# Scores of q and k from high and low parts: three fp32r matmuls in place of one fp32 matmul, twelve heads

## What is computed

```
qh = partial_rope(rms_norm(q.reshape(shp), q_norm_g), positions) * (HEAD_DIM ** -0.5)
kh = partial_rope(rms_norm(k.reshape(shp), k_norm_g), positions)
...
s = jnp.einsum('bnqrhe,bnkrhe->bnrhqk', qb, kn)
```

## Time and profile before

| | |
|---|---|
| time, median of 3 runs (lowest to highest) | 3410.15 us (3408.2 to 3416.05) |
| profiled execution, its own time | 3404.39 us |
| its span | 3403.1 us |
| busy: PE, DVE, ACT | 99%, 67%, 49% |
| heads' stretch of the trace | about 98 to 363 us |

### The profile page before, as it was taken

One profiled execution on the slowest core, in us unless ns is written; L12 is line 12 of the kernel. 1 busy time (PEld: TensorE's weight loads), 2 busy tenths in 40 slices (PEclk: granted clock), 3 DMA queues, 4 the chain that ended last, 5 costly groups with the idle time before them and its releaser, 6 DMA issues.

```text
span 3403.1 us, 66505 instructions
## 1 busy us (share of the span) xinstructions
PE 3372.4 (99%) x29362; PEld 3352.6 (99%) x29362; DVE 2284.4 (67%) x3021; ACT 1664.2 (49%) x1788; POOL 136.0 (4%) x132
## 2 busy tenths in 40 slices
PE   8999999999999999999999999999999999999999
PEld 8999999999999999999999999999999999999998
DVE  5777679986655555545555587778646778787456
ACT  5555434455544444343443454333445667777455
POOL 0000000144400000000000000000000000000000
PEclk9999999999999999999999999999999999999999
DMA  6435455566676666655566655555555545555543
GB/s 248 164 140 181 176 218 186 186 213 212 218 237 221 213 220 209 227 195 190 198 220 215 209 177 203 194 194 182 208 189 177 195 162 198 199 186 186 211 174 137
DMA packets 125328, 669.45 MB, mean 197 GB/s; under 512 B 11056, under 2 KB 44592, under 8 KB 47344
## 3 DMA queue, kind: packets, MB, share of 16 engines
q1 hardware_dynamic: 88224, 623.44, 52.2%
q10 hardware_dynamic: 36816, 41.75, 3.7%
HBM read 643.39 MB, written 20.97 MB: 195 GB/s over the span
## 4 chain that ended last, share of the span: by engine, by line
PE 94%; DVE 3%; ACT 1%; issue 1%; DMA 1%; ACTq 0%; SPq 0%; DVEq 0%
PE PS L553 30%; PE PS L554 30%; PE PS L555 30%; PE PS L848 2%; DVE WL L1538 1%; ACT WH L1039 1%; DMA RAW<-in_w_in 0%; DVE WX L1538 0%; DVE A L1562 0%; PE PS L743 0%; PE PS L728 0%; DVE OO L2081 0%; PE PS L568 0%; DVE XT L2087 0%; PE PS L830 0%
## 5 line engine op out<-in xcount | busy, mean ns | idle before, releaser
L1538 DVE TENSOR_TENSOR WL<-RAW,WH 128x2048 fp32r<-128x2048 f32 x579 | 1325.4, 2290 | 832.1 <-ACT WH L1039 829.9
L553 PE MATMUL PS<-A,WH 128*128 128x256 f32 x5536 | 1545.5, 279 | 18.2 <-DVE WL L1544 9.8
L554 PE MATMUL PS<-A,WH 128*128 128x256 f32 x5536 | 1532.1, 277 | 0.0
L555 PE MATMUL PS<-A,WL 128*128 128x256 f32 x5536 | 1531.9, 277 | 0.0
L1039 ACT ACTIVATE WH<-RAW 128x2048 fp32r<-128x2048 f32 x579 | 1107.6, 1914 | 846.4 <-PE PS L555 830.5
L553 PEld LDWEIGHTS PS<-A,WH 128*128 128x128 f32 x5536 | 1042.2, 188 | 23.0 <-DVE WL L1544 9.8
L554 PEld LDWEIGHTS PS<-A,WH 128*128 128x128 f32 x5536 | 1040.9, 188 | 0.6
L555 PEld LDWEIGHTS PS<-A,WL 128*128 128x128 f32 x5536 | 1040.4, 188 | 0.0
L553 PE MATMUL PS<-CO,WH 128*128 128x256 f32 x2048 | 565.2, 276 | 0.0
L554 PE MATMUL PS<-CO,WH 128*128 128x256 f32 x2048 | 565.2, 276 | 0.0
L555 PE MATMUL PS<-CO,WL 128*128 128x256 f32 x2048 | 565.2, 276 | 0.0
(11 more groups left out here) (294 smaller groups left out, 2903.9 us busy)
## 6 DMA issues: line engine op xcount, KB each, us to landing
RAW<-in_w_in SPq DMA_DIRECT2D x175, 1024.0 KB, 4.8
RAW<-in_peer_down SPq DMA_DIRECT2D x128, 1024.0 KB, 4.8
RAW<-in_peer_up SPq DMA_DIRECT2D x128, 1024.0 KB, 5.4
RAW<-in_w_out SPq DMA_DIRECT2D x80, 1024.0 KB, 4.7
RAW<-in_w_gate SPq DMA_DIRECT2D x32, 1024.0 KB, 4.8
RAW<-in_w_query SPq DMA_DIRECT2D x16, 1024.0 KB, 4.8
gates_away<-XT ACTq DMA_DIRECT2D x16, 1024.0 KB, 8.2
RAW<-in_pool_w SPq DMA_DIRECT2D x16, 1024.0 KB, 4.7
```

Source lines behind the costliest of these rows:

```text
L553: e.matmul(ps, wh, x[:, k, 0, :], start=first, stop=False, skip_group_check=True)
L554: e.matmul(ps, wh, x[:, k, 1, :], start=False, stop=False, skip_group_check=True)
L555: return e.matmul(ps, wl, x[:, k, 0, :], start=False, stop=last, skip_group_check=True)
L1538: e.tensor_tensor(W_LOW[c], RAW[:, c % NRAW, :], W_HIGH[c].bitcast(F32), ALU.subtract).then_inc(s_lo, 1)
```

## The change

The score step of each head no longer multiplies q and k as fp32. A new ACT step `qh` rounds the rotated q and k to fp32r in SQH; a new DVE step `ql` subtracts, which gives the low parts in SQL; `p2` then does three fp32r matmuls for each half of the queries, and waits for `ql` where it waited for `r3`. SQH and SQL are the buffers of the squares, so `sh` of the next head now waits for the scores of the head before. In `pe_out` the steps of head 11 and the split of chunk 3 move.

```diff
@@ att_pe
         if x == "p2":
-            e.wait_ge(AD[w].sem, AD[w].at(("r3", h)))
+            e.wait_ge(AD[w].sem, AD[w].at(("ql", h)))
             e.wait_ge(AA[w].sem, AA[w].at(("vn", h)))
             for qt in range(2):
-                ins = e.matmul(BANK[6][:, qt * T:qt * T + T], QKV[:, s, 0, qt * 128:qt * 128 + 128], QKV[:, s, 1, :],
-                               start=True, stop=True, skip_group_check=True)
+                for n, (q, k) in enumerate(((SQH, SQH), (SQH, SQL), (SQL, SQH))):
+                    ins = e.matmul(BANK[6][:, qt * T:qt * T + T], q[:, qt * 128:qt * 128 + 128], k[:, T:2 * T],
+                                   start=(n == 0), stop=(n == 2), skip_group_check=True)
@@ pe_out
-        parts = [(0, 0, 14), (1, 0, 14), (2, 0, 14), (3, 0, 6), (0, 14, 16), (1, 14, 16), (2, 14, 16), (3, 6, 16)]
+        parts = [(0, 0, 14), (1, 0, 14), (2, 0, 14), (3, 0, 9), (0, 14, 16), (1, 14, 16), (2, 14, 16), (3, 9, 16)]
...
-                if n == 28:
+                if n == 33:
                     att_pe(e, "p2", 11)
-                if n == 40:
+                if n == 44:
                     att_pe(e, "p3", 11)
-                if n == 44:
+                if n == 48:
                     att_pe(e, "p4", 11)
@@ att_act
             if h:
-                e.wait_ge(AP[1 - w].sem, AP[1 - w].at(("ss", h - 1)))
+                e.wait_ge(AP[1 - w].sem, AP[1 - w].at(("qk", h - 1)))
...
+        if x == "qh":
+            e.wait_ge(AD[w].sem, AD[w].at(("r3", h)))
+            e.activation(SQH[:, :].rearrange("p (a t) -> p a t", a=2), QKV[:, s, 0:2, :], ACT.Copy).then_inc(
+                AA[w].sem, AA[w].one(("qh", h)))
@@ act_first
                 if j == 0 and h >= 1:
                     att_act(e, "rt", h - 1)
+                if j == 1 and h >= 1:
+                    att_act(e, "qh", h - 1)
@@ att_dve
+        if x == "ql":
+            e.wait_ge(AA[w].sem, AA[w].at(("qh", h)))
+            e.tensor_tensor(SQL[:, :].rearrange("p (a t) -> p a t", a=2), qk,
+                            SQH[:, :].bitcast(F32).rearrange("p (a t) -> p a t", a=2), ALU.subtract).then_inc(
+                S.sem, S.one(("ql", h)))
@@ dve_first
                 if j == 0 and h >= 2:
                     att_dve(e, "rc", h - 2)
+                if j == 2 and h >= 1:
+                    att_dve(e, "ql", h - 1)
                 lo_to(e, c + 2)
```

More of the change, by code:

```diff
@@ L414, in build @@
     ap_n = two(("ss", "vt", "qk", "pt", "pv"))
-    aa_n = two(("sq", "sh", "ln", "rs", "vn", "e0", "e1", "pt"))
-    ad_n = two(("sl", "nq", "nk", "r1", "r2", "r3", "sm", "mx", "rc", "m0", "m1", "hi", "lo"))
+    aa_n = two(("sq", "sh", "ln", "rs", "vn", "qh", "e0", "e1", "pt"))
+    ad_n = two(("sl", "nq", "nk", "r1", "r2", "r3", "ql", "sm", "mx", "rc", "m0", "m1", "hi", "lo"))
     s_ones = sem("ones_rounded")
@@ L1199, in act_out @@
         hi_to(e, C_WO + 3)
+        att_act(e, "qh", 11)
         att_act(e, "ex", 11)
@@ L1780, in dve_out @@
         att_dve(e, "ro", 11)
+        att_dve(e, "ql", 11)
         att_dve(e, "sm", 11)
```

## The result

The changed kernel takes 3419.36 us in the median of 20 runs (3414.67 to 3426.43), the kernel before on the same chip 3413.55 (3406.49 to 3422.58, 20 runs). The ratio is 1.0020 with a 95% interval of 1.0013 to 1.0027: slower by 6.8 us (4.4 to 9.2). Measured a second time, in eight new runs, it was 3415.87 us, ratio 1.0026 (1.0015 to 1.0036), or 8.9 us (5.1 to 12.3). One of ten executions of the kernel before in that second session took 5200.5 us at a granted clock of 0.61 and is left out of every comparison.

What follows compares the result with a forecast made beforehand. PE, busy in 3372.4 of 3403.1 us, bounds the kernel. Waits less work 4.2, ring 2.0, carried lateness 1.9, weight loads 0.6 and tail 0.7 make +9.4 us: 3419.5 us from a median of 3410.15, range 3413 to 3426.

Steps and rivals of the forecast that it cites:

- The ring: Heads 9 to 11: ACT and DVE alternate in a 20.5 us loop, outside PE's 19.45 us period; +2.0 us.
- Waits at the scores: Heads 0 to 10: PE waits for q and k, ready later behind qh and ql; 6.5 us in sum.
- PE's work: Scores cost PE 0.69 us a head against 0.88, -2.3 us; weight loads not hidden at waits, +0.6 us.
- The tail: End of pe_out: the chunk after the first four has three blocks less cover and waits; +0.7 us.
- Carried lateness: Heads before the ring binds: lateness is carried on in part from head to head; +1.9 us.
- Waits alone: Rival: no ring binds, only score waits and small terms cost; +4.2 to +5.5 us, 3414 to 3416; chance 0.20.
- All hidden: Rival: q and k ready when PE needs them, only the 2.3 us work gain counts; 3407.9 us; chance 0.06.
- Ring and GLA: Rival: in heads 3 to 8 GLA's steps add a 1 us wait in each; +15 us, 3425; chance 0.10.
- The clock: Rival: short repeated idling drops PE to 1.2 GHz for one head, up to 19 us, 3439; chance 0.03.

Runs made afterwards that it cites:

- the run with the product alone: Kernel before with the scores made by six fp32r matmuls a head on the normalised input, no qh, ql or new wait; ratio 1.0004.
- the run with another bank: Changed kernel with PSUM banks of the output projection's first and fourth chunks swapped; 283.11 us from head 0's first q evacuation to the output projection's transposes, one execution.
- the one with the longer ring: Changed kernel with an unused ACT copy of 0.6 us behind the exponentials of each head; ratio 1.0023.
- the new steps alone: Changed kernel with qh and ql computed and waited for, but the scores again fp32 products of q and k; ratio 1.0029.

## Why the prediction was right, and where a step was off

The forecast was 3419.5 us, slower by 9.4; measured were 3419.36 us and ratios that make 6.8 and 8.9 us, and 8.84 and 9.03 in two pairs of traces. That the time itself is met to 0.2 us is luck: in the same 20 runs the kernel before took 3413.55 us, 3.4 more than the 3410.15 that the forecast started from, and the difference of the two medians is 5.8 us and not 9.4. The first ratio's interval ends at 9.2. The direction and the mechanism hold, and by the traces the sum does to 0.6 us. The terms hold less well than the sum.

- **The ring: right.** Forecast 20.5 us, measured 20.40, and the missing 0.1 is the start of the high part 0.54 us behind `qh` where 0.66 was taken. It binds from head 8 to 9 on, as forecast. Four runs stand behind it: the period ignores PE's work, grows with an ACT copy inside the ring, outlasts a later place of the scores, and vanishes when `qh` stands one place further back on ACT.
- **Waits at the scores: right in kind, high in size.** Heads 0 and 5 wait longest, as forecast, and seven steps wait where "some ten" were forecast; 6.9 us lies at the low end of 7 to 10. In terms of the sum, the idle time forecast was 6.5 + 2.0 + 1.9 + 0.7 = 11.1 us; PE's idle time grew by 8.04. Some 1.5 us of the difference is only where it is counted: the forecast goes by starts, the profile lets a wait begin when the last matmul's record ends, 0.28 us after its start, where without a wait the next one starts after 0.12. The other 1.6 us are waits that came out short, head 1's 0.1 for 0.4 and those of heads 9 and 10 among them. A slip of the sum goes the other way: the ring's term takes off a wait of 0.6 us for each of heads 9, 10 and 11, but at head 11 none had been counted, so by its own rule the sum was up to 0.6 us higher, 10.0.
- **PE's work: the term that was mis-sized.** Forecast was -2.3 + 0.6 = -1.7 us; busy time grew by 0.80. Where the scores wait for nothing six starts take 0.72 us, for 0.69 forecast, and with the slow first matmul behind the fp32 product gone the gain is 0.14 us a head, 1.7 in all for 2.3. Where PE waits in front of them they take 0.82, and so they do at head 4, where it waits for 0.03 us, and at head 6, where the profile shows no wait. That is ten heads, where two were delayed in this way before: 0.8 us more, for the 0.6 forecast. The 1.5 us of records in front of waits, counted as waiting in the forecast, stand in the busy time too. Together that is -1.7 + 0.8 + 1.5 = 0.6 of the 0.80. The pace of the stream is not the reason in the changed kernel: 638 and 695 distances are slow in its two profiles, 699 and 745 before. It is in the run with the product alone, which gained 0.47 us of busy time and nothing in the stretch. So the misses of the two terms, 3.1 us of idle time too many and 2.5 of busy time too few, have opposite signs: 1.5 us is one and the same quantity counted on either side, and that the rest cancels as well as it does is luck.
- **A wait that was not forecast**: the output projection's first chunk waits 1.31 us for its bank, 0.56 before. It was in the waits of PE of the kernel before and was passed over; the run with another bank shows it to be PE's debt to the ring in another place. The transposes of head 0 (L739) wait 1.3 us for 0.5 in the first profile; in the second it is 0.13 and no such line stands, since PE, at half the clock, came there later.
- **The tail: right.** 0.58 us at the chunk after the first four, for 0.7.
- **Carried lateness: right.** 5.5 us at head 7 and 6.0 at head 8, for 5.1 and 5.6 (the measured ones hold the 0.36 us that was there at the start).

The rivals. Waits alone fell: it gave 4.2 to 5.5 us, which the first ratio by itself would allow, but the traces have 8.84 and 9.03, and the ring was shown. All hidden fell with the waits, and even its gain of 2.3 us isn't there in the one run of the product alone. Ring and GLA would have been +15; the waits of heads 3 to 8 never passed 1.57 us. The clock: at head 0, window of the changed kernel around the longest wait,

```profile
118.00:122.00 4.00, 1.93 (x16) 1.94 (x17) 2.53 (x4) 3.31 (x4) 0.00 (x0) 1.00 0.63 250
```

PE is busy in under half of 4 us and the granted clock is 1.00, the level of 2.4 GHz, here and in the whole stretch of this profile. That isn't so in every one. Five profiled executions have a wait of 2.4 to 2.5 us at head 0. In three (this one, the one with the longer ring, the one with another bank) the clock stayed at 1.00, and in two (the second profile of the changed kernel and the new steps alone) it was 0.50, the level of 1.2 GHz, for 3.4 us, from 0.35 us ahead of the wait's end in the one and from 0.83 us behind it in the other. A wait of 2.36 us in front of the output projection, in the run with the scores three blocks later, left it at 1.00. So the mechanism of this rival is real, and its price was not: the stretch lost nothing, since PE had 1.3 us of waiting in hand right behind, and nowhere else in the stretch did the clock fall. (Far behind it, between 2705 and 2735 us, every profile has 3.4 to 6.8 us at 0.50, behind waits that are 1.7 and 3.2 us long in the kernel before.) The Trainium skill (TensorE: Matmul & The Clock Gate, "A second HAM failure mode: psum-queue depth-cycling") tells of micro-idling that makes the clock swing; here a single wait of 2.4 to 2.5 us was followed by the lower clock in two of five traces, and the waits of 0.4 to 1.7 us in the stretch in none.

## What to carry to other kernels

A step that is put into an in-order queue costs more than its own time if what stands behind it was ready earlier: look at what the engine would have done in the idle time in front of the new step, and sum the chain from that step round to its next occurrence. If that sum exceeds the period of the engine that bounds the kernel, every repetition pays the difference; moving the step one place back, or to the engine that makes its input, takes it away. And a gain on the bounding engine that is a few per cent of a period should be measured alone, and more than once, before it is put into a sum. One profile of a kernel can miss what its next one shows: here the split into busy and idle time, and a fall of the clock.

## What the hardware showed that was not expected

**The stream of matmuls has two paces at one granted clock.** Records of the same form (128x128 weights, 256 columns, fp32r, a weight load each) follow each other by 113.3 or by 117.8 ns in means over twelve, at a granted clock of 1.00. In the traces, but for one place in the first profile of the kernel before (at 2720 us, behind a stretch at the lower clock), the pace changes only where the stream is interrupted, by a wait or by other matmuls; it can hold for tens of microseconds. Near the attention it takes mostly the same values in the same places from profile to profile of one kernel. Far behind it the same wait of 1.03 us, at 2047 us, left 117.8 ns behind it in one profile of the changed kernel and 113.3 in the other. Neither kind of product for the scores brings one pace: the fp32 product turned slow into quick at heads 8 and 10 of the kernel before and quick into slow at head 9, and in the kernel with both steps on DVE the fp32r matmuls turned slow into quick at head 8. 4% of a 20 us window are 0.8 us, which is more than many an edit is worth. The Trainium skill (TensorE: Matmul & The Clock Gate, "Wait — 56ns, not 53.3ns?") gives the columns at 2.4 GHz and about 2.5 ns on top, an estimate of 109.2 ns for 256 columns; both measured paces lie above it, and for this stream the measurement decides. What sets the pace stays open.

**A conversion of 128x512 to fp32r is quicker on DVE than on ACT**, 0.43 us against 0.63. DVE timeline at head 8 of the kernel with both steps on DVE:

```profile
296.33 0.43 DVE L1707 CAST SQH<-QKV 128x512 fp32r<-128x512 f32 x1
296.79 0.69 DVE L1709 TENSOR_TENSOR SQL<-QKV,SQH 128x512 fp32r<-128x512 f32 x1
```

There `ql` ends 1.19 us after the rotation; through ACT it ended 1.39 us after it (302.36 against 300.97).
